# Both softmax attentions of a decoder block as one stage over head pairs, in plain fp32

## What is computed

```python
h = rmsnorm(x, norm_g); proj = h @ w_in
# gated linear attention: 4 heads, chunks of 64 tokens
# FoX: 6 heads of 64, causal, 2048 keys
s = einsum('bhqd,bhkd->bhqk', qb, kh) * 64 ** -0.5
s = s + cb[..., :, None] - c[..., None, :]        # c = cumsum(log_sigmoid(forget gate))
p = softmax(where(mask, s, -inf)); o_fox = einsum('bhqk,bhkd->bhqd', p, vh)
# memory attention: 4 heads of 64, no mask, 256 keys
s = einsum('bthd,bmhd->bhtm', q, mk) * 64 ** -0.5; p = softmax(s)
o_mem = einsum('bhtm,bmhd->bthd', p, mv)
# each group is multiplied by a SiLU gate
return rmsnorm(x + concatenate([o_gla, o_fox, o_mem]) @ w_out, final_norm_g)
```

## Time and profile before

| | |
|---|---|
| time, median of 3 (lowest, highest) | 1479.8 us (1478.74, 1481.03) |
| span of the profiled execution | 1480.9 us |
| busy: PE, DVE, ACT, POOL | 1312.8, 665.6, 576.9, 411.6 us |
| linear attention, its instructions from about | 632 to 812 us |
| memory heads | 812 to 916 us |
| FoX heads | 916 to 1288 us |
| output projection | 1288 to 1481 us |

### The profile page before, as it was taken

The page is one execution under the profiler, slowest core; times in us unless marked ns, Lnnn a source line. Parts: engine busy times, 40 slices in busy tenths (PEclk is TensorE's granted clock), DMA queues, the critical chain, the costliest instruction groups (busy, mean ns, idle before and its releaser), DMA issues. The chain is left out here.

```text
span 1480.9 us, 20787 instructions
## 1 busy us (share of the span) xinstructions
PE 1312.8 (89%) x6576; PEld 1053.3 (71%) x6576; DVE 665.6 (45%) x1606; ACT 576.9 (39%) x1154; POOL 411.6 (28%) x408
## 2 busy tenths in 40 slices
PE   5898989999999999938785985999899999599997
PEld 4887878888888888814453663777678687478886
DVE  4563311110000011178874763888788798432222
ACT  3563201111111000047652874777677777421010
POOL 5223420111111011044553577222322422300000
PEclk9999999999999999959876987999999999799999
DMA  5453333331222121165321543422623520355553
GB/s 201 144 164 118 111 111 113 127 120 64 70 78 78 64 78 58 49 177 166 109 85 60 165 113 84 115 93 61 156 63 94 122 59 12 98 207 198 199 174 137
DMA packets 98908, 166.45 MB, mean 112 GB/s; under 512 B 10740, under 2 KB 51444, under 8 KB 96996
## 3 DMA queue, kind: packets, MB, share of 16 engines
q1 hardware_dynamic: 96088, 156.97, 34.7%
q10 hardware_dynamic: 2560, 8.39, 1.4%
q0 software_dynamic: 192, 0.33, 0.1%
HBM read 101.36 MB, written 64.29 MB: 112 GB/s over the span
## 5 line engine op out<-in xcount | busy, mean ns | idle before, releaser
L644 PE MATMUL col_cps<-h_T,tok_slot 128*128 128x512 f32 x2112 | 481.6, 390 | 4.0 <-POOL tok_slot L600 3.9
L644 PEld LDWEIGHTS col_cps<-h_T,tok_slot 128*128 128x128 f32 x2112 | 397.9, 188 | 87.8 <-issue 4.9
L1736 PE MATMUL out_yps<-out_w,out_mix 128*128 128x512 f32 x768 | 177.7, 394 | 19.3 <-DMA out_mix<-scr_mix 16.8
L1736 PEld LDWEIGHTS out_yps<-out_w,out_mix 128*128 128x128 f32 x768 | 145.7, 190 | 51.1 <-DMA out_mix<-scr_mix 17.1
L1540 ACT ACTIVATE fox_pT<-fox_tps 128x512 fp32r<-128x512 f32 x240 | 124.8, 531 | 88.2 <-PE fox_tps L1473 85.5
L1578 DVE TENSOR_SCALAR_CACHE_REDUCE fox_prob<-fox_sps 128x512 f32<-128x512 f32 (+2 forms) x240 | 142.0, 606 | 36.6 <-PE fox_sps L1463 33.7
L1589 DVE TENSOR_TENSOR fox_pT<-fox_tps,fox_pT 128x512 fp32r<-128x512 f32 x240 | 141.6, 604 | 21.7 <-ACT fox_pT L1540 20.9
L1473 PE MATMUL fox_tps<-all_ident,fox_prob 128*128 128x128 f32 x816 | 134.6, 278 | 15.1 <-ACT fox_prob L1532 8.2
L707 DVE COPY tok_xn<-col_cps 128x512 f32<-128x512 f32 x24 | 16.6, 692 | 287.4 <-PE col_cps L644 287.4
L1486 PE MATMUL fox_ops<-fox_pT,fox_v 128*128 128x512 f32 x480 | 137.2, 376 | 0.0
L1473 PEld LDWEIGHTS fox_tps<-all_ident,fox_prob 128*128 128x128 f32 x816 | 99.9, 141 | 45.1 <-ACT fox_prob L1532 11.6
(11 more groups left out here) (189 smaller groups left out, 1760.3 us busy)
## 6 DMA issues: line engine op xcount, KB each, us to landing
scr_split<-tok_w SPq DMA_DIRECT2D x64, 256.0 KB, 2.7
out_mix<-scr_mix SPq DMA_DIRECT2D x32, 512.0 KB, 4.2
tok_xin<-in_w_cols SPq DMA_DIRECT2D x22, 512.0 KB, 3.8
tok_xin<-in_x SPq DMA_DIRECT2D x16, 512.0 KB, 3.7
scr_gates<-tok_xn SPq DMA_DIRECT2D x32, 256.0 KB, 2.3
out_x<-in_x SPq DMA_DIRECT2D x16, 512.0 KB, 6.2
out<-out_o ACTq DMA_DIRECT2D x16, 512.0 KB, 4.9
scr_fox_v<-tok_vst SPq DMA_DIRECT2D x16, 384.0 KB, 2.9
```

The source lines that it names most:

```text
L644: mm = nc.tensor.matmul(cps[c][:, :], w[s][a_][:, kk, :], hT[b_][:, kk, c * CH:(c + 1) * CH], start=(kk == 0 and n == 0), stop=(kk == KT - ...
L1736: mm = nc.tensor.matmul(yps[s][:, c, :], mix[s][a][:, kk, :], w[b][:, kk, c * CH:(c + 1) * CH], start=(kk == 0 and n == 0), stop=(kk == MI ...
```

## The change

The two softmax stages become one function, `attention`, over 40 jobs: `JOBS` lists 16 for the memory heads (2 pairs of heads times 8 groups G of 256 queries), then 24 for FoX (3 pairs times 8 groups). Nothing in it is a hardware loop. Queries, keys, values and probabilities are plain fp32 and nothing is split, except the stage's output, which the output projection still wants in two parts. The two heads of a pair sit in rows 0 to 63 and 64 to 127. Their score matmuls use 64 rows each, into two PSUM banks; their weighted sums use 128 rows and write output partitions 0 to 63 and 64 to 127 of one bank (64 columns of the array each), and so do the spread sums.

FoX's offsets are added on DVE: `crow` is broadcast to all partitions, POOL adds the mask for the diagonal block (`diagonal`), and DVE makes scores plus offsets and their running minimum with `tensor_tensor_reduce`. `plan(n)` sets which score tiles of job n+1 go into each key step m of job n (all within three quarters of the steps), and when ACT takes its exponentials. The transposed probabilities are only copied, in even steps by DVE and in odd ones by ACT. The weighted sum lags two steps. A job's first transpose waits for all exponentials of the job, of both tiles of 128 queries; before, each transpose of a turn's first step waited for its own tile.

In the other stages: queries and keys leave PSUM with one copy on ACT in place of a copy and a subtraction; memory keys and values and FoX values likewise; the `first_fill` memsets on DVE in the linear attention go; half of the scratch stores of queries and keys go.

```diff
@@ -24,6 +24,12 @@
 MEM_H = 4
 MIX_T = 8
 
+FOX_PAIRS, MEM_PAIRS = FOX_H // 2, MEM_H // 2
+QG = 256
+QSLOTS = 3
+JOBS = ([(False, p, G) for p in range(MEM_PAIRS) for G in range(T // QG)]
+        + [(True, p, G) for p in range(FOX_PAIRS) for G in range(T // QG)])
+
 TOK_C = FOX_H * DH + FOX_H + GLA_R
 FGLR = FOX_H + GLA_R
 NSPLIT, NGATE, NRAW = 8, 8, 6
@@ -46,14 +52,14 @@
...
-                            act.wait_ge(stored[c % 2], j * split_st + (c // 2) * 32)
-                            nc.scalar.activation(stage[c % 2][HI][:, :], cps[c][:, :], ACT.Copy).then_inc(hi_done, 1)
-                act.wait_ge(bank_free, 4 * NSPLIT + 4)
+                            act.wait_ge(stored[c % 2], j * plain_st + (c // 2) * 16)
+                            nc.scalar.activation(plain[c % 2][:, :], cps[c][:, :], ACT.Copy).then_inc(bank_free, 1)
...
-                with dve.Fori(0, NSPLIT // 2) as h:
-                    for s in range(2):
-                        for c in range(NCH):
-                            j = 2 * h + s
-                            dve.wait_ge(hi_done, 4 * j + c + 1)
-                            nc.vector.tensor_tensor(stage[c % 2][LO][:, :], cps[c][:, :],
-                                                    stage[c % 2][HI][:, :].bitcast(F32), ALU.subtract
-                                                    ).then_inc(bank_free, 1)
...
-                for stage in next_stages:
-                    stage.first_fill(nc.vector)
...
+    def plan(n):
+        ahead = list(score_units(n + 1)) if n + 1 < NJ else []
+        units, done, tiles_done, out = n_keys[n], 0, 0, []
+        for m in range(units):
+            upto = min(len(ahead), -(-len(ahead) * (m + 1) * 4 // (3 * units)))
+            ready = 0
+            if ahead:
+                upto_exp = upto if m + 1 == units else done
+                ready = sum(1 for t in range(2) if all(u[0] > t for u in ahead[upto_exp:]))
+            out.append(([(k, ahead[k]) for k in range(done, upto)], list(range(tiles_done, ready))))
+            done, tiles_done = upto, max(tiles_done, ready)
+        return out
...
+    def by_act(k):
+        return k % 2 == 1
...
+                def scores(n, u, k):
+                    fox, p, G = JOBS[n]
+                    t, c, w = u
+                    if t == 0 and c == 0:
+                        pe.wait_ge(tiles.q_loaded[n % QSLOTS], 16 * (n // QSLOTS + 1))
+                        if fox:
+                            pe.wait_ge(tiles.pair_loaded[p % 2], 48 * (p // 2 + 1))
+                        else:
+                            pe.wait_ge(tiles.mem_loaded, 16 * 2 * MEM_PAIRS)
+                    if k >= 2:
+                        pe.wait_ge(minned, score_ends[k - 2])
+                    for e in range(2):
+                        rows = slice(DH * e, DH * (e + 1))
+                        keys = tiles.k[p % 2][rows, c * CH:c * CH + w] if fox else tiles.mem_k[rows, p, 0:w]
+                        mm = nc.tensor.matmul(sps[k % 2][e][:, 0:w], tiles.q[n % QSLOTS][rows, t * P:(t + 1) * P],
+                                              keys, start=True, stop=True)
+                    mm.then_inc(scored, 1)
...
+                def transposes(n, m):
+                    fox, p, G = JOBS[n]
+                    k = first_key[n] + m
+                    if k >= 2:
+                        if by_act(k):
+                            pe.wait_ge(copied_act, copied_by(k - 2, True))
+                        else:
+                            pe.wait_ge(copied_dve, copied_by(k - 2, False))
+                    if m == 0:
+                        pe.wait_ge(expd, first_exp[n + 1])
+                    for t in range(1 if fox and m == 2 * G + 1 else 0, 2):
+                        for e in range(2):
+                            mm = nc.tensor.transpose(tps[k % 2][:, e, t * P:(t + 1) * P],
+                                                     prob[n % 2][:, t, e, m * P:(m + 1) * P], ident[:, :])
+                    mm.then_inc(transposed, 1)
...
+                def weigh(n, m):
+                    fox, p, G = JOBS[n]
+                    k = first_key[n] + m
+                    if m == 0 and n >= 2:
+                        pe.wait_ge(gated, n - 1)
+                    if by_act(k):
+                        pe.wait_ge(copied_act, copied_by(k, True))
+                    else:
+                        pe.wait_ge(copied_dve, copied_by(k, False))
+                    lo = P if fox and m == 2 * G + 1 else 0
+                    for e in range(2):
+                        rows = slice(DH * e, DH * (e + 1))
+                        values = tiles.v[p % 2][:, m, rows] if fox else tiles.mem_v[:, p, m, rows]
+                        mm = nc.tensor.matmul(ops[n % 2][rows, 0, lo:QG], values, pT[k % RINGP][:, e, lo:QG],
+                                              start=(m == 0), stop=(m == n_keys[n] - 1), skip_group_check=True)
+                    mm.then_inc(weighed, 1)
+
+                def spread_sums(n):
+
+                    pe.wait_ge(inverted, n + 1)
+                    if n >= 2:
+                        pe.wait_ge(gated, n - 1)
+                    for t in range(2):
+                        for e in range(2):
+                            mm = nc.tensor.matmul(ops[n % 2][DH * e:DH * (e + 1), 1, t * P:(t + 1) * P],
+                                                  rinv[n % 2][:, 2 * t + e:2 * t + e + 1].to_broadcast([P, DH]), ident[:, :],
+                                                  start=True, stop=True, skip_group_check=True)
+                    mm.then_inc(spread, 1)
+
+                for k, u in enumerate(score_units(0)):
+                    scores(0, u, k)
+                waiting = []
+                for n in range(NJ):
+                    for m, (ahead, _) in enumerate(plan(n)):
+                        transposes(n, m)
+                        for x, u in ahead:
+                            scores(n + 1, u, first_score[n + 1] + x)
+                        waiting.append((n, m))
+                        if len(waiting) > LAG:
+                            nn, mm_ = waiting.pop(0)
+                            if mm_ == 0:
+                                spread_sums(nn)
+                            weigh(nn, mm_)
...
+                def exponentials(n, t):
+                    act.wait_ge(minned, minima_until(n, t))
+                    last = len(minima_list(n, t)) - 1
+                    for x, (k0, w) in enumerate(pieces(n, t)):
+                        for e in range(2):
+                            pr = prob[n % 2][:, t, e, k0:k0 + w]
+                            nc.scalar.activation(pr, pr, ACT.Exp, bias=nmin[n % 2][:, 2 * t + e, last:last + 1], scale=-1.0,
+                                                 accum_out=rsum[n % 2][:, 2 * t + e, x:x + 1]).then_inc(expd, 1)
+
+                def copy(n, m):
+                    fox, p, G = JOBS[n]
+                    k = first_key[n] + m
+                    act.wait_ge(transposed, k + 1)
+                    if k >= RINGP:
+                        act.wait_ge(weighed, k - RINGP + 1)
+                    lo = P if fox and m == 2 * G + 1 else 0
+                    nc.scalar.activation(pT[k % RINGP][:, :, lo:QG], tps[k % 2][:, :, lo:QG], ACT.Copy).then_inc(copied_act, 1)
+
+                for t in range(2):
+                    exponentials(0, t)
+                for n in range(NJ):
+                    for m, (_, ready) in enumerate(plan(n)):
+                        if by_act(first_key[n] + m):
+                            copy(n, m)
+                        for t in ready:
+                            if t == 0 and n >= 1:
+                                act.wait_ge(summed, n)
+                            exponentials(n + 1, t)
...
+                    done = score_ends[k] - 2 * len(minima(n, t, c, w))
+                    for k0, width, on_diag in minima(n, t, c, w):
+                        x = minima_list(n, t).index((k0, width, on_diag))
+                        if x:
+                            dve.wait_ge(minned, done)
+                        for e in range(2):
+                            ps = sps[k % 2][e][:, k0 - c * CH:k0 - c * CH + width]
+                            pr = prob[n % 2][:, t, e, k0:k0 + width]
+                            acc = nmin[n % 2][:, 2 * t + e, x:x + 1]
+                            if fox:
+                                ck = (diag[n % 2][:, e, t * P:(t + 1) * P] if on_diag
+                                      else tiles.c[p % 2][:, e, k0:k0 + width])
+                                nc.vector.tensor_tensor_reduce(
+                                    pr, ps, ck, -SCALE, nmin[n % 2][:, 2 * t + e, x - 1:x] if x else 3e38,
+                                    ALU.add, ALU.min, acc).then_inc(minned, 1)
+                            else:
+                                nc.vector.tensor_scalar(pr, ps, -SCALE, None, ALU.mult, ALU.min, accum_out=acc
```

(14 more changed lines are left out.)

696 lines of the change are left out of this document (257 added, 439 removed).

## The result

The changed kernel takes 1544.78 us (median of 4, 1541.46 to 1551.19) beside 1480.41 for the kernel before on the same chip: ratio 1.0442, 95% interval 1.0413 to 1.0471, 64 us slower. The prediction said 1525 us, 1466 to 1602, slower with chance 0.80.

A forecast was written before the change was run, and what follows sets the result against it. PE was taken as the bound, DVE close behind: 1480.9 - 464 (old stages) + 503 (422 PE work, 37 + 39 waits, 5 first job) + 18 clock - 10.6 gains elsewhere = 1527, called 1525 us; range 1466 to 1602, forecast's own 1495 to 1550.

The forecast's parts named there:

- change of shape: PE switching between whole array, 64 rows and 64 columns in each step: 0.15 to 0.20 us each, 102 us together.
- a sign of being wrong: Prediction called itself wrong if PE's waits for exponentials were under 40 us or the shape changes were hidden.
- Rival 3: Score matmuls on row halves do not overlap on PE: scores cost 101 us more, 1610 us; chance 0.10.
- Rival 2: DVE becomes the bound in steps with scores, by a slow new instruction: 1575 us; chance 0.12.
- DVE's 280 us: DVE's work in the new stage: 312 new instructions, 104 copies and the finish, about 280 us, under PE.
- Waits for exponentials: PE waiting at job starts for all exponentials: 37 us in FoX and 39 us in the memory jobs.
- The memory part: The stage's sixteen memory jobs: 6.25 us a job, plus 5 us for the first job and 10 us for clock.
- 8 for FoX: Clock loss in the FoX jobs: 8 us, beside 10 us for the memory jobs, 18 together.
- Gains elsewhere: Savings outside the new stage: tail 5.8, memsets 3.3, fewer evictions 1.5, together 10.6 us; column stage nothing.
- The memsets' 3.3: Linear attention: without three DVE memsets the waiting mask product starts earlier, 3.3 us gained.
- The tail: From the stage's last PE instruction to the next stage's load: 6.2 us in place of 12.0, 5.8 gained.
- Rival 1: Job-start waits close and the clock stays: 30 us of 81 left, 452 us stage, 1458 us, faster; chance 0.15.

The follow-up runs named there:

- e1_pairs: Changed kernel with PE taking a job's key steps two at a time (both transposes, then scores, then both sums): 1530.6 us.
- e4_all: Changed kernel with three edits: key steps in pairs, copies off ACT where exponentials are due, next job's scores within half of the steps: 1466.8 us.
- e14_single: e11_mended with the key steps one by one and not in pairs: 1456.2 us.
- e11_mended: e4_all with next job's first scores before the waiting transposes, scores within three quarters of steps, some loads moved, POOL's offsets two jobs ahead in three buffers: 1435.4 us.
- e5_whole_scores: Changed kernel with each score matmul on all 128 rows, so the two of a pair can't run side by side: 1609.4 us.

## Why the prediction was right, and where its sum was off

**Side: right. Mechanism: right in the waits, in part in the work.** PE waits at the start of jobs, and the edits that shortened these waits gained. PE's timeline shows each change of shape at its price, 102 us by count. But the prediction named it a sign of being wrong if they were hidden, and in part they are: taking half of them out gave FoX nothing in `e1_pairs` and `e4_all`, and 21 us of 47 between `e14_single` and `e11_mended`. That they cost the changed kernel 102 us is not shown. The time was 20 us over the forecast, inside its own range of 1495 to 1550.

**The unit prices held.** 1.17 us for a step of transposes and sums, 0.85 of streaming for a pair of score tiles at 512 columns (1.06 with its change), 0.10 to 0.15 at each change, 686 for the new instruction's first form (688), and 6.25 for a memory job (6.03 at the upper clock level). `e5_whole_scores` shows 1.81 us for a pair of score tiles on the whole array against 1.06 in halves. The Trainium skill (TensorE: Matmul & The Clock Gate, on packing small matmuls) gives 3.07 times the speed for four row tiles at once; the run agrees that row tiles overlap, here with two. Rival 3 gave 1610 for serial halves, and that kernel took 1609.4, in part by luck: the rival put 85 us on 1525, and the measured 64.6 stand on 1544.8.

**Two sums of the prediction don't hold.** Rival 2's 1575 doesn't follow from its terms: 80 stretches at 1.0 us more on 1525 give 1605 before any longer chain. And DVE's 280 us left out the memory heads' minima and 20 copies, as said above.

**Waits for exponentials:** 66.5 us against 76 predicted for 37 + 39.

**The memory part:** 115 predicted, 112.0 measured.

**The term that was too small is FoX beyond its 37 us of waits.** "For memory jobs at 0.80 I add ... 10 us in all, and 8 for FoX: 18." FoX took 435.6, where the sum leaves 406 (521 - 115): 361 of work, 37 of waits, 8 for the clock. Measured are 47.9 of waits, 31.5 for exponentials and 16.4 for ACT's copies of odd steps that stand behind exponentials: the prediction counted them in a job with group 1 and in the memory jobs, but gave the long jobs no such wait. That is 11 of the 29 us missing. The other 19 are in PE's busy time, 387.5 us. The waits in the FoX jobs of the changed kernel, and the window of the FoX jobs in `e14_single`, whose changes of shape are as many:

```profile
PE att_tps L1391 <- ACT att_prob L1451: 31.5, 16, 2.8
PE att_tps L1391 <- ACT att_pT L1461: 16.4, 9, 3.0
```

```profile
871.00:1256.40 385.40, 368.61 (x2394) 177.67 (x2392) 279.51 (x879) 165.66 (x334) 57.93 (x75) 1.00 0.17 51
```

At a clock of 1.00 the busy time is 368.6, near the 361, so the work was priced about right and its stretching was not. A clock of 0.95 means 44 of 435.6 us at the lower level and costs 22 us at most, an estimate from the granted clock, where 8 were put. The sums' weight loads wait 42 us for copies too, which the prediction didn't count. How much each gives no run parts.

**Gains elsewhere:** 14.8 in this one trace, 10.6 predicted. The memsets' 3.3 can't be seen in it: the linear attention takes 176.1 us from its first matmul to the next stage, where it took 175.5. In the other runs, whose code is the same up to there, it takes from 171.2 to 176.8, and the new stage starts from 798.1 to 805.4 us. So this length scatters by more than the term, and 6.6 is the least gain ahead of the stage in any of these traces. Before, the last memset ended at 663.3 and the mask product waited behind it, but PE was at its own work from 656.98 to 667.9 and only later rows need that product. The tail gave 8.2 and not 5.8 (5.1 us from PE's end to the next load, 12.0 before). 6.6 came in the token and column stages, where 1.5 was put for the token stage and nothing for the column stage: it ends at 620.9 and not 628.3, 2.9 of it from an earlier start, the rest with 2.8 us less of waiting for POOL's slots and a half-clock stretch of 3.4 us at 192.4 us that is gone.

**Rival 1,** that the waits can close, was wrong for this kernel and right about the design: at 452 us for the stage it gave 1458, and `e14_single`, which keeps every change of shape, has 455.7 and 1456.2. `e11_mended`, with pairs, has 434 and 1435. It took edits of order and one more buffer, no arithmetic.

## What to carry to other kernels

Price a change of array shape (0.10 us without streaming and an uncovered weight load, as measured here) like an instruction, but look at what else runs in the gap before paying to remove it: 47 us of them were worth nothing, then 21, as the other engines' stalls went. When one engine does both the copies that release PE and the long operations for the next job, the order of its queue is the first thing to change: 41 us here for one rule on who copies. Issue the first independent work of the next job ahead of the wait, and then check every producer two steps back (here POOL's offsets), since here each lead that PE gained uncovered the next late engine.
